# Six norms of a diffusion backbone: where the squares of eight tiles are added, and how the factors are spread

## The reference

```
y = x * rsqrt(mean(x * x, axis=-1) + 1e-6) * g
input = y * (1 + scale) + shift        # scale, shift, gate from the condition
h = h + w * gate * f(input)
```

## Time and profile before

| what | us |
|---|---|
| median of three runs | 1719.74 |
| lowest and highest run | 1719.39, 1721.28 |
| span of the profiled execution, first to last instruction | 1717.1 |
| TensorE busy with matmuls in it | 1660.1 |
| VectorE, ScalarE, GpSimd busy | 1067.5, 578.3, 81.3 |

### The profile page before, as it was taken

One profiled execution on the slowest core, in us unless ns is written; L12 is line 12 of the kernel. 1 busy time (PEld: TensorE's weight loads), 2 busy tenths in 40 slices (PEclk: granted clock), 3 DMA queues, 4 the chain that ended last, 5 costly groups with the idle time before them and its releaser, 6 DMA issues.

```text
span 1717.1 us, 25878 instructions
## 1 busy us (share of the span) xinstructions
PE 1660.1 (97%) x9927; PEld 1589.1 (93%) x9927; DVE 1067.5 (62%) x1803; ACT 578.3 (34%) x751; POOL 81.3 (5%) x48
## 2 busy tenths in 40 slices
PE   8899999988899899999989999998999998999998
PEld 4899999988756899999989999998999998999998
DVE  3677668767754766767966777697745435334323
ACT  2423232253344442322234333222642325333222
POOL 1200000034100100000010000001000001000000
PEclk9999999989999899999989999999999998999999
DMA  9755547526200445555634545564533332433332
GB/s 310 187 182 164 192 159 244 170 85 207 77 1 31 157 146 173 177 189 196 224 120 135 193 161 195 190 226 157 186 124 96 125 123 85 136 122 122 124 130 77
DMA packets 222917, 261.81 MB, mean 152 GB/s; under 512 B 14502, under 2 KB 207494, under 8 KB 222854
## 3 DMA queue, kind: packets, MB, share of 16 engines
q1 hardware_dynamic: 222854, 260.95, 46.3%
HBM read 258.64 MB, written 2.29 MB: 152 GB/s over the span
## 4 chain that ended last, share of the span: by engine, by line
PE 86%; issue 6%; DVE 4%; ACT 1%; POOL 1%; DMA 0%; POOLq 0%; SPq 0%; ACTq 0%; DVEq 0%
PE ps L1066 15%; PE ps L1067 15%; PE ps L1069 15%; PE ps L1022 9%; PE ps L1024 9%; PE ps L1023 9%; PE ps L1055 3%; PE ps L1037 2%; PE ps L1257 1%; DVE macc L754 1%; PE ps L1126 1%; PE ps L1294 1%; POOL hrs L503 1%; PE ps L1363 1%; DVE w_lo L731 1%
## 5 line engine op out<-in xcount | busy, mean ns | idle before, releaser
L731 DVE TENSOR_TENSOR w_lo<-raw,w_hi 128x2048 fp32r<-128x2048 f32 x164 | 380.0, 2317 | 282.3 <-ACT w_hi L527 282.2
L1066 PE MATMUL ps<-x_hi,w_hi 128*128 128x384 f32 x1536 | 523.3, 341 | 13.2 <-ACT x_hi L553 9.9
L1067 PE MATMUL ps<-x_hi,w_lo 128*128 128x384 f32 x1536 | 520.1, 339 | 0.0
L1069 PE MATMUL ps<-x_lo,w_hi 128*128 128x384 f32 x1536 | 517.1, 338 | 0.0
L527 ACT ACTIVATE w_hi<-raw 128x2048 fp32r<-128x2048 f32 x169 | 322.9, 1911 | 344.2 <-PE ps L1024 326.3
L754 DVE SCALAR_TENSOR_TENSOR macc<-mraw,cT,macc 128x256 f32<-128x256 f32 x896 | 359.9, 478 | 0.0
L1066 PEld LDWEIGHTS ps<-x_hi,w_hi 128*128 128x128 f32 x1536 | 292.1, 190 | 17.0 <-issue 13.3
L1067 PEld LDWEIGHTS ps<-x_hi,w_lo 128*128 128x128 f32 x1536 | 292.1, 190 | 0.0
L1069 PEld LDWEIGHTS ps<-x_lo,w_hi 128*128 128x128 f32 x1536 | 291.3, 190 | 0.0
L1022 PE MATMUL ps<-act_hi,w_hi 128*128 (+1 forms) x832 | 281.8, 339 | 0.0
L1024 PE MATMUL ps<-act_hi,w_lo 128*128 (+1 forms) x832 | 279.6, 336 | 0.0
(11 more groups left out here) (154 smaller groups left out, 1310.7 us busy)
## 6 DMA issues: line engine op xcount, KB each, us to landing
raw<-ffn_w_gu SPq DMA_DIRECT2D x88, 1024.0 KB, 5.1
mraw<-mod_w SPq DMA_DIRECT2D x66, 1024.0 KB, 7.4
raw<-ffn_w_down SPq DMA_DIRECT2D x44, 1024.0 KB, 4.8
raw<-sgu_w_in SPq DMA_DIRECT2D x16, 1024.0 KB, 5.5
raw<-attn_w_in SPq DMA_DIRECT2D x9, 1024.0 KB, 5.0
raw<-sgu_w_out SPq DMA_DIRECT2D x8, 1024.0 KB, 4.8
mfirst<-mod_w SPq DMA_DIRECT2D x6, 1024.0 KB, 12.8
raw<-attn_w_out SPq DMA_DIRECT2D x4, 1024.0 KB, 4.9
```

Of the source, the lines that this page charges most:

```text
L731: nc.vector.tensor_tensor(w_lo[q0 % 2][:, :], raw[q0 % 2][:, :], w_hi[q0 % 2][:, :].bitcast(F32), ALU.subtract).then_inc(lo_done, 1)
L1066: mm(out, hi[:, cols], x_hi[:, k, :], start=(k == 0), stop=False)
L1067: mm(out, lo[:, cols], x_hi[:, k, :], start=False, stop=False)
L1069: last = mm(out, hi[:, cols], x_lo[:, k, :], start=False, stop=(k == KD - 1))
```

## The change

GpSimd now adds the squares of all eight tiles (seven additions in place of three), and TensorE sums only that one tile, three matmuls in place of fifteen. The diagonal and its product with ones are gone: TensorE transposes, for each block of 128 tokens, a view that repeats a column of `rs` 128 times. `rms` on VectorE thus issues the two halves of the low part with nothing between them. The waits follow: ScalarE's first four squares of a norm no longer wait for the sums of the norm before, its last four wait for the same additions as before, under new counts.

```diff
--- before.py
+++ after.py
@@ -473,15 +473,15 @@
 
             def norm(n):
 
-                for k in range(1, 4):
+                for k in range(1, KD):
                     pool.wait_ge(sq_done, KD * n + k + 1)
                     if k == 1:
                         if n:
-                            pool.wait_ge(rb_done, n)
+                            pool.wait_ge(stat_done, n)
                         nc.gpsimd.tensor_tensor(sqsum[:, :], sq[:, 0, :], sq[:, 1, :], ALU.add).then_inc(acc_done, 1)
                     else:
-                        pool.wait_ge(acc_done, 3 * n + k - 1)
-                        nc.gpsimd.tensor_tensor(sqsum[:, :], sqsum[:, :], sq[:, k, :], ALU.add).then_inc(acc_done, 1)
+                        pool.wait_ge(acc_done, 7 * n + k - 1)
+                        nc.gpsimd.tensor_tensor(sqsum[:, :], sqsum[:, :], sq[:, k % 4, :], ALU.add).then_inc(acc_done, 1)
                 pool.wait_ge(ms_done, n + 1)
                 nc.gpsimd.tensor_tensor(rs[:, :], ms[:, :], mhalf[:, 0:TT], ALU.pow).then_inc(rs_done, 1)
 
@@ -533,9 +533,7 @@
                     if k == 1 and block:
                         act.wait_ge(msum_done, block - MOD_SUM)
                     if k >= 4:
-                        act.wait_ge(acc_done, 3 * n + max(1, k - 4))
-                    elif n:
-                        act.wait_ge(stat_done, n)
+                        act.wait_ge(acc_done, 7 * n + max(1, k - 4))
                     nc.scalar.activation(sq[:, k % 4, :], h[:, m, :], ACT.Square).then_inc(sq_done, 1)
 
             def make_x(n, j):
@@ -792,10 +790,6 @@
                 if q is not None:
                     dve.wait_ge(hi_done, q + 1)
                     half(0)
-                dve.wait_ge(rs_done, n + 1)
-                nc.vector.tensor_tensor(sqsum[:, :].rearrange("p (a q) -> p a q", a=TT),
-                                        ident[:, None, :].to_broadcast([P, TT, P]),
-                                        rs[:, :, None].to_broadcast([P, TT, P]), ALU.mult).then_inc(diag_done, 1)
                 if q is not None:
                     half(1).then_inc(lo_done, 1)
 
@@ -1115,22 +1109,17 @@
 
             def norm_sums(n):
 
-                for k in (4, 5, None, 6, 7):
-                    if k is None:
-                        pe.wait_ge(acc_done, 3 * n + 3)
-                    else:
-                        pe.wait_ge(sq_done, KD * n + k + 1)
-                    for t in range(TT):
-                        part = sqsum[:, P * t:P * t + P] if k is None else sq[:, k % 4, P * t:P * t + P]
-
-                        last = mm(ps[:, 4, t:t + 1], part, ones[:, 0:1], start=(k == 4 and t == 0), stop=(k == 7),
-                                  skip_group_check=True)
+                pe.wait_ge(acc_done, 7 * n + 7)
+                for t in range(TT):
+                    last = mm(ps[:, 4, t:t + 1], sqsum[:, P * t:P * t + P], ones[:, 0:1], start=True, stop=True)
                 last.then_inc(stat_done, 1)
 
             def norm_spread(n):
 
-                pe.wait_ge(diag_done, n + 1)
-                mm(ps[:, 5, 0:T], ones[:, :], sqsum[:, :], start=True, stop=True).then_inc(rb_done, 1)
+                pe.wait_ge(rs_done, n + 1)
+                for t in range(TT):
+                    last = nc.tensor.transpose(ps[:, 5, P * t:P * t + P], rs[:, t:t + 1].to_broadcast([P, P]), ident[:, :])
+                last.then_inc(rb_done, 1)
 
             def ffn(f, n):
                 q = Q_F[f]
```

## The result

The changed kernel is slower by a ratio of 1.0016, with a 95% interval of 1.0009 to 1.0023 (20 runs of either; median 1723.51 us, 1721.03 to 1725.82, against 1721.32, 1717.19 to 1722.12). By the ratio that is about 2.8 us, between 1.5 and 4.0; the two medians are 2.2 apart. The forecast was 5.6 us slower; the sign and the range hold, the size is half, and it stays under the 0.2% that I had called distinguishable. Twenty runs told it all the same.

What follows compares the result with a forecast made beforehand. TensorE, busy 97% of the span, was taken to bound the kernel, through its norm chains: 4.59 (norms 1, 4, 5) + 0.36 + 0.27 + 0.44 = 5.66, say 5.6 us, 1719.7 + 5.6 = 1725.3; own range 1722.5 to 1728, 8 in 10 1721.0 to 1731.5.

Steps and rivals of the forecast that it cites:

- The bound: At each norm one chain between TensorE's sub-layers; what the change does to it goes into the time one for one.
- The additions: GpSimd's four more per norm, at a pitch of 1.16 us, end behind all squares; TensorE's sums and VectorE's `ms` wait.
- The sums: TensorE's three remaining matmuls, at half clock with a weight load: 1.58 us; `ms` 2.85 later in norms 1, 4, 5.
- Norm 0: Told apart from the others: matmuls 0.82 us later, spread 0.38 shorter, so 0.44 slower, with 0 as lower bound.
- The rival of the clock that is still full: Sums and transposes run at full clock: 5.4 us gone, about 1719.9 us, no change; chance 0.11.
- The spread: From the power's end to the first product: three transposes at half clock take 0.92 us, a saving of 1.32 per norm.
- that rival: TensorE's transposes load the repeated view slowly: 1.79 us more in five norms, 14.5 in all, 1734.2; chance 0.06.
- The power: On GpSimd, still meeting the first half panel on VectorE: left at 1.77 us, 2.01 from the start of `ms`.
- the rival of waiting for both: GpSimd's power waits for both VectorE half panels: 1.13 us more in five norms, 11.3 in all, 1731.0; chance 0.14.
- The other side: Clock returns sooner in the first panel behind each norm, making the change a gain, up to 1713.5 us; chance 0.05.

Runs made afterwards that it cites:

- e1: The changed kernel with the old spread (diagonal and its product with ones) put back, so the additions alone: 1730.99 us, ratio 1.0064 to the kernel before.
- e2: The kernel before with the three transposes alone, its additions and fifteen sums kept: 1712.89 us, ratio 0.9962 to the kernel before.
- e5: The kernel before with the three transposes, VectorE's first half panel moved behind the power and the second behind two products: 1709.20 us, ratio 0.9937.
- e7: The kernel before with the three transposes and four GpSimd additions, TensorE summing `sqsum` and the three last tiles: 1709.62 us, ratio 0.9941.
- e6: The kernel before with the three transposes, half panels moved behind power and products, useless matmuls before (5) and behind (12) the transposes: 1702.91 us, ratio 0.9900.

## Why the prediction was right, and what was off

- **The bound** was right for norms 1 to 5. They are on the path one for one: the shifts read in the rows are 10.5 and 6.7 us, and the runs of either part alone say 11 and 6.5. With norm 0 the rows make 3.5 us, and the runs say 2.8 (1.5 to 4.0).
- **The additions** were right in mechanism: they end behind the squares, and TensorE and then VectorE wait for them. e1 gives the term by itself, 11 us. The pitch was 1.14 in place of 1.16 ((6.72 - 1.00) / 5), 0.09 less for each norm.
- **The sums** are the term that was mis-sized. I took 1.58: half clock, and 0.16 for a first weight load after the pause. The six took 1.44, 1.44, 1.40 and 1.44 in norms 2 to 5, so over the 1.42 of the earlier trace rows a first weight load added at most 0.02 here. In norm 1 most of them ran at full clock:

```profile
355.75 0.99 PE L1114 MATMUL ps<-ones,sqsum 128*128 128x1 f32 x6 [4.79 <-POOL sqsum L484]
```

  That is 0.59 less. With the pitch these make the 11.82 into 10.48; against them stands 0.24 in norm 2, whose additions paused once.
- **Norm 0** was the second term off: -0.3 in place of +0.44. I had carried half clock over to a norm in which TensorE waits for only 3.17 us; its sums took 0.80, 0.78 less than I took. That 0.44 - 0.78 is just the -0.34 of the rows is chance: TensorE gained 1.0 up to the end of the spread, and 0.7 were lost again in the wait for ScalarE, which stood behind a weight panel. The prediction has no transfer on this path. The rival of the clock that is still full came true for the sums of norm 0 and most of those of norm 1, and for the transposes of norms 1 to 5 nowhere. In norm 5 the clock fell only 0.7 us ahead of the sums, so half clock there was right by a narrow margin.
- **The spread** was right to 0.02 us per norm: 0.90 for the transposes against a forecast of 0.92, 3.00 from `ms` to the product. e2 gives 6.5 us for it, forecast 6.6. The view that repeats a column loads no slower than an ordinary one at full clock (0.54 against 0.53 for three); that rival is out.
- **The power** was right: 1.77 in all five norms, although both halves were queued. GpSimd got in, and VectorE lost nothing either (2.35 for two halves, 1.21 for one). That refutes the rival of waiting for both, and with it the strict reading of "SBUF — State Buffer" in the Trainium skill ("SBUF: two separate sides"), by which a second half that starts ahead of the power would hold it off; 2.9 would have been seen. That the power waits for the first half agrees with that page: e5 has 0.86 without it, against 1.77. That the second half lost nothing beside the power doesn't agree with its full blocking of the other; what either engine held, and when, no row shows.
- **The other side**, a clock that comes back sooner, did not happen: 23.2 us at half clock behind the restarts against 24.1, where 2.2 in each of five norms would have been needed.
- **The chances.** I gave 0.73 to slower by over 0.2% and 0.22 to a change within it; the 0.16% lies in the second, with an interval up to 0.23%, and at the lower end of the forecast's own range (2.8 to 8.3 us). The forecast of 0.33% was too far up by 2.2 us of terms in the rows (1.4 in norms 1 to 5, 0.8 in norm 0). Of the 0.7 us between the rows' 3.5 and the runs' 2.8 nothing can be said; it lies within the interval.

## What to carry over

When work is moved from a busy engine to an idle one, ask when the last piece of it ends against what the busy engine would do meanwhile. With four additions on GpSimd the kernel was 3.6 us faster than with three, and the last three of the seven cost 12.9 (e7 beside e2 and the changed kernel). Two opposed terms of 0.6% and 0.4% look like a change that does nothing, and running each part by itself shows that one is worth keeping. Before tuning the links of a wait on TensorE, look what the wait does to its clock, for the half clock behind it may be worth more than the links.

## What was not expected of the hardware

- Useless matmuls in TensorE's waits make this kernel faster: the granted clock stays at 1.00 through norms 1 to 5, worth 0.66% to the changed kernel, while 24 of them ahead of the sums alone are worth 0.12%, hardly more than the noise.
- Thirty one-column rows, 3.5 us of unbroken work for TensorE, were followed by a fall of the clock in e6 though the next matmuls stood ready. In the kernel before it fell even amid the sums of norm 2.
- Two VectorE instructions with two inputs each, back to back beside a GpSimd power, cost GpSimd 0.91 us and VectorE nothing (2.35 for both, 1.21 for one).
